# One gelu instruction for two rows' dot products in the expert phase

## The reference, cut to what matters

```
act = gelu(einsum('thkd,td->thk', u[expert], x))      # one dot product per chosen expert
out = einsum('thk,thkd->td', gate * act, v_emb[expert])
```

## Time and profile before

| | |
|---|---|
| median of 3 runs | 3348.26 us (3347.88 to 3351.38) |
| profiled execution | 3351.4 us, of which span 3349.7 us |
| expert phase's first to last row | 745 to 3340 us of the span |
| busy, share of the span | TensorE 82%, VectorE 71%, ScalarE 68%, GpSimd 41% |
| granted TensorE clock, mean | 0.914 |
| gathers (software queue) | 1001 MB, 74.0% of the 16 engines' span |

### The profile page before, as it was taken

The page is one execution under the profiler, slowest core; times in us unless marked ns, Lnnn a source line. Parts: engine busy times, 40 slices in busy tenths (PEclk is TensorE's granted clock), DMA queues, the critical chain, the costliest instruction groups (busy, mean ns, idle before and its releaser), DMA issues.

```text
span 3349.7 us, 47831 instructions
## 1 busy us (share of the span) xinstructions
PE 2730.9 (82%) x16625; PEld 2067.2 (62%) x16625; DVE 2386.9 (71%) x5661; ACT 2272.8 (68%) x4096; POOL 1388.5 (41%) x1158
## 2 busy tenths in 40 slices
PE   8999989889987887787778677776688878878985
PEld 6777667765665664554665454555566658767654
DVE  5554445466788985676776667899988899877556
ACT  3222553236778886786987777767888886887777
POOL 0000100034544553444544443445456654566764
PEclk9999999999999899889789889998899987897997
DMA  3001143149999999999999999999999998999998
GB/s 115 25 33 38 64 139 126 63 164 408 417 418 420 411 415 420 420 414 420 418 407 420 420 415 420 411 418 398 419 365 384 372 359 306 348 400 390 407 399 321
DMA packets 198354, 1099.19 MB, mean 328 GB/s; under 512 B 33767, under 2 KB 49415, under 8 KB 77704
## 3 DMA queue, kind: packets, MB, share of 16 engines
q0 software_dynamic: 152064, 1001.19, 74.0%
q1 hardware_dynamic: 46050, 94.97, 7.9%
HBM read 1173.94 MB, written 11.54 MB: 354 GB/s over the span
## 4 chain that ended last, share of the span: by engine, by line
DMA 24%; DVE 16%; PE 15%; ACT 14%; issue 7%; POOL 2%; DVEq 0%; POOLq 0%; ACTq 0%
DMA early_rows<-in_uv,choice_index 12%; PE expert_acc L3539 7%; DVE scores L3045 5%; DMA rows<-in_uv,expert_sk 3%; ACT early_rows L3231 3%; DMA early_rows<-in_uv,expert_sk 3%; ACT rows L3231 3%; DMA rows<-in_uv,choice_index 2%; DMA rows<-in_uv,scores 2%; DVE early_rows L3045 2%; ACT expert_wt L3225 2%; ACT L3223 2%; DMA early_rows<-in_uv,scores 1%; ACT L1920 1%; ACT expert_wt L3223 1%
## 5 line engine op out<-in xcount | busy, mean ns | idle before, releaser
L3539 PE MATMUL expert_acc<-ident,rows 128*128 128x128 f32 x4072 | 622.1, 305 | 277.7 <-ACT rows L3231 276.2
L3539 PEld LDWEIGHTS expert_acc<-ident,rows 128*128 128x128 f32 x4072 | 524.5, 158 | 471.7 <-ACT rows L3231 421.5
L3539 PE MATMUL expert_acc<-ident,early_rows 128*128 128x128 f32 x4096 | 601.7, 297 | 238.2 <-ACT early_rows L3231 235.8
L3539 PEld LDWEIGHTS expert_acc<-ident,early_rows 128*128 128x128 f32 x4096 | 503.9, 153 | 440.1 <-ACT early_rows L3231 389.4
L3231 ACT ACTIVATE early_rows<-early_rows,expert_wt 128x1024 f32<-128x1024 f32 x512 | 588.6, 1150 | 16.7
L3231 ACT ACTIVATE rows<-rows,expert_wt 128x1024 f32<-128x1024 f32 x510 | 586.2, 1149 | 16.6
L3223 ACT ACTIVATE expert_wt<-expert_dot 128x1 f32<-128x1 f32 x1024 | 202.5, 198 | 484.4 <-DVE expert_dot L3045 479.9
L2029 POOL DMA_INDIRECT rows<-in_uv,choice_index x256 | 317.7, 1241 | 397.1 <-PE expert_acc L3539 353.1
L2029 POOL DMA_INDIRECT early_rows<-in_uv,choice_index x256 | 321.7, 1257 | 338.7 <-PE expert_acc L3539 293.8
L3045 DVE CUSTOM_DVE_ANT_0 rows<-rows,expert_xn 128x1024 f32<-128x1024 f32 x256 | 312.9, 1222 | 149.2 <-DMA rows<-in_uv,choice_index 148.5
L3045 DVE CUSTOM_DVE_ANT_0 early_rows<-early_rows,expert_xn 128x1024 f32<-128x1024 f32 x256 | 312.8, 1222 | 124.1 <-DMA early_rows<-in_uv,choice_index 122.0
(11 more groups left out here) (518 smaller groups left out, 5112.9 us busy)
## 6 DMA issues: line engine op xcount, KB each, us to landing
H<-in_x SPq DMA_DIRECT2D x8, 1024.0 KB, 10.7
expert_w_raw<-in_w_pq SPq DMA_DIRECT2D x16, 512.0 KB, 10.9
stick_w_raw<-in_w_feat SPq DMA_DIRECT2D x8, 512.0 KB, 3.4
tok_w_raw<-in_w_tok SPq DMA_DIRECT2D x8, 512.0 KB, 3.3
out_w_raw<-in_w_out SPq DMA_DIRECT2D x8, 512.0 KB, 3.5
mkv_w_raw<-in_w_mk SPq DMA_DIRECT2D x16, 256.0 KB, 4.0
mkv_w_raw<-in_w_mv SPq DMA_DIRECT2D x16, 256.0 KB, 3.0
pq_w_raw<-in_w_mq SPq DMA_DIRECT2D x8, 512.0 KB, 3.4
```

The source lines that it names most:

```text
L3539: last_mm = nc.tensor.matmul(acc[:, k * P:(k + 1) * P], rows[R % ROWS][:, D + k * P:D + (k + 1) * P], co.ident[:, :], start=b >= dense.FIR ...
```

## The change

For rows below 1020 the gelu is issued at even rows alone, for two neighbouring columns of the dot tile, and it waits until both dot products are there. The Copy with the gate and the scaling of the row stay one for each row. The last four rows are done as before. All else is untouched.

```diff
-                        act.wait_ge(dots, TOPK * g + r + 1)
-                        link(nc.scalar.activation(wt[:, s, 0, r:r + 1], dot[:, s, r:r + 1], ACT.Gelu))
                         R = TOPK * g + r
+                        pairs = R < NB * BLOCK - 4
+                        if not pairs or r % 2 == 0:
+                            n = 2 if pairs else 1
+                            act.wait_ge(dots, R + n)
+                            link(nc.scalar.activation(wt[:, s, 0, r:r + n], dot[:, s, r:r + n], ACT.Gelu))
                         link(nc.scalar.activation(wt[:, s, 1, r:r + 1], wt[:, s, 0, r:r + 1], ACT.Copy,
                                                   scale=row_gate[:, r:r + 1]))
```

## The result

The changed kernel takes 3429.23 us (median of 4 runs, 3426.35 to 3433.81); the kernel before, on the same chip, 3349.77 (3347.88 to 3351.38). The ratio is 1.0241, 95% interval 1.0229 to 1.0253: slower by 79 us, where 8 were forecast.

The account below looks back on a forecast made before the run. DMA bounds 745 to 2460 us and from 2900, ScalarE and VectorE to 2700, VectorE to 2900. Terms 1 + 0 + 0 + 4.4 + 2 + 0.75 = +8.2 on 3348.3 give 3356 us; range 3341 to 3371.

Parts of the forecast that it names:

- the cover: 745 to 1000 us: the DMA covers most of VectorE's added waiting for TensorE's scores; +1 us, ends 0 and +11.
- 1000 to 2460: Stretch with a 14.4 us queue, shortened by 2 us: nothing on the path; 0, from -2 to +4 us.
- 2460 to 2700: Stretch with ScalarE 89% busy: VectorE's wait at L2848 stays as it is; 0, ends -11 and +18 us.
- the turn of the ring: From 2460 us, in the upper bounds only: 1.4 us of lateness for every eight rows, +18 in 2460 to 2700.
- rival C: 2460 to 3100 us: the ring's turn limits wherever the queue is short; +24 us, 3372; chance 0.13.
- 2700 to 3100: Two stretches with longer L2908 waits: +4.4 us up to 2900, then +2 with the DMA hiding the greater part.
- The end: Last rows: row 1020's gelu and the sum's copy come later, nothing parallel; +0.75 us, ends 0 and 1.5.
- The pair's price: ScalarE's gelu of two columns costs 0.20 us, like a single column's; bounds 0.19 and 0.30.
- one pair of table loads fewer: At about 1550 us one pair of ScalarE's table loads falls away, 2.6 us under the DMA; counted as nothing.
- the size of L2908's wait: 2700 to 3100 us: seven L2908 waits each 1.46 us longer, 4.4 us up to 2900 and 5.8 after.
- the sign: Whole kernel: the change makes it slower, by 8.2 us in sum.
- The gain: ScalarE saves 112 us, nearly all beside idle time; at most 11 us could count, in 2460 to 2700.

Follow-up runs that it names:

- ring7: The kernel before with a ring of seven rows instead of eight, single gelus; 3387.14 us, ratio 1.0107.
- pair_relaxed: The changed kernel with four of VectorE's interposed jobs due one or two rows later; 3394.59 us, ratio 1.0138.
- bare: The kernel before and the changed kernel, both without the stick-breaking arithmetic of rows 2 to 200; rows 0 to 192 take 507.3 and 510.9 us.
- relaxed: The kernel before with four of VectorE's interposed jobs due one or two rows later; 3345.99 us, ratio 0.9994.
- odd_pairs: The changed kernel with pairs beginning at odd rows, rows 0 and 15 of each 16 single; 3425.86 us, ratio 1.0234.
- side_first: The changed kernel with ScalarE's interposed work at even rows ahead of the wait for both dot products; 3457.94 us, ratio 1.0319.
- pair_0_448: The changed kernel with pairs in rows 0 to 447 only; 38.4 us late at row 192 and 55.7 at row 448.
- wait_only: The changed kernel with its wait for both dot products but one single-column gelu for each row; 3442.3 us, ratio 1.0269.
- pair_448_736: The changed kernel with pairs in rows 448 to 735 only; +5 us against the kernel before.
- pair_736_1020: The changed kernel with pairs in rows 736 to 1019 only; +20 us against the kernel before.
- bare_single: The kernel before, single gelus, without the stick-breaking arithmetic of rows 2 to 200; rows 0 to 192 take 507.3 us.

## Why the prediction was wrong

**The step that failed** is the cover: "The gathers keep 414 GB/s through those waits today, so the DMA covers most: +1", and for 1000 to 2460 us "a queue of 14.4 us shortened by 2 us stays 12 us long, nearly five rows. Nothing is on the path: 0". By row 96 after is 19.7 us late, by row 640 48.8.

The queue did shorten by 2 us (14.4 to 12.0; in 745 to 1000, where the prediction had no such number, from 11.0 and 10.7 to 9.8 and 9.9), but two things the step held apart work together. The queue's 12 us is a median. And the lateness that shortens it also makes VectorE stand, during which no row is used up and no gather issued. The timeline of after shows two such chains, from row 4 on (start, duration, engine, line; the lines between are left out):

```profile
754.33 1.22 DVE L3045 CUSTOM_DVE_ANT_0 rows<-rows,expert_xn 128x1024 f32<-128x1024 f32 x1 [1.28 <-DMA rows<-in_uv,choice_index]
755.59 0.20 ACT L3227 ACTIVATE expert_wt<-expert_dot 128x2 f32<-128x2 f32 x1 [4.13 <-DVE expert_dot L3045]
759.14 0.49 PE L3437 MATMUL expert_side<-expert_above,ident 128*128 128x128 f32 x2
759.66 0.70 ACT L3147 ACTIVATE expert_w_raw<-expert_side 128x640 f32<-128x640 f32 x1 [2.36 <-PE expert_side L3437]
760.40 0.50 DVE L2935 TENSOR_SCALAR expert_w_raw<-expert_w_raw 128x640 f32<-128x640 f32 x1 [1.29 <-ACT expert_w_raw L3147]
...
764.92 0.09 DVE L3045 DVE_READ_ACCUMULATOR2_ANT expert_dot<- 128x1 f32 x1
773.52 0.69 DVE L2927 TENSOR_TENSOR scores<-expert_acc,rstd 128x512 f32<-128x512 f32 x1 [8.50 <-PE expert_acc L3421]
776.54 0.20 ACT L3227 ACTIVATE expert_wt<-expert_dot 128x2 f32<-128x2 f32 x1 [10.73 <-DVE expert_dot L3045]
781.14 0.99 POOL L2029 DMA_INDIRECT early_rows<-in_uv,choice_index  x1 [8.49 <-PE expert_acc L3542]
```

The pair's gelu waits for row 5's dot product of 754.33. VectorE loses 1.29 us at L2935, with no wait there in the kernel before: it waits for ScalarE's tanh L3147, and that for TensorE's L3437 of 759.14, which before started at 756.99. This lateness comes from row 0. TensorE in after, and then in before:

```profile
747.18 1.97 PE L3542 MATMUL expert_acc<-ident,early_rows 128*128 128x128 f32 x8 [6.68 <-ACT early_rows L3234]
748.94 3.62 PE L3412 MATMUL expert_acc<-z_b,mix_b 128*128 128x512 f32 x4
```

```profile
748.11 2.49 PE L3409 MATMUL expert_acc<-z_b,mix_b 128*128 128x512 f32 x4
```

Row 0 is scaled 3.56 us after its own dot product where before it was 2.02, which is the wait for row 1, 1.54 us. TensorE starts on it after 6.68 us without work (before 5.14), and its granted clock is 0.52 from 747 to 753 (before 0.67 from 746 to 751; 1.00 behind that in both), so the four matmuls behind row 0 take 3.62 us for 2.49. TensorE then works without a gap, and its step for L3147 is late by both, 2.85 us by its distance from row 0's dot product.

The second chain is longer. An even row's dot product is there at 765.00, but its gelu comes at 776.54, since before its partner's turn VectorE stands 8.50 us for TensorE's scores (before, 6.37 us at the same place, with row 8 already on its way). GpSimd waits 8.49 us for that row's slot and issues at 781.14. The kernel before, same row: gelu and gather.

```profile
765.03 0.20 ACT L3223 ACTIVATE expert_wt<-expert_dot 128x1 f32<-128x1 f32 x1 [1.13 <-DVE expert_dot L3045]
...
773.06 0.99 POOL L2029 DMA_INDIRECT early_rows<-in_uv,choice_index  x1 [2.56 <-PE expert_acc L3539]
```

So the lateness of a row is 1.4 to 2 us only where its partner follows at the rows' pace. Where VectorE's own wait lies between the two, the row bears all of it, here 11.5 us, and the queue with it. The forecast took the size of the one for all.

How much that costs in the queue can be counted from the packets, rows 8 to 640 (my count: time with so many gathers issued and not yet landed, and the bytes moved in it; the 25 us of before that are missing lie nearly all at seven):

```
gathers outstanding        0     1     2     3     4     5     6
before  us                 -     -    42   229   425   565   410
        GB/s               -     -   390   405   412   420   420
after   us                 6    42   188   454   596   419    38
        GB/s              27   270   356   406   416   420   419
```

Against 420 GB/s throughout, before loses 20 us in these rows and after 70: the difference of 50 is the 48.8 us by which row 640 is late. So up to there the loss is bytes not moved while three gathers or fewer stood in the queue.

**Which of the two it is.** Shorter queue with the old stalls: +37 (ring7). Longer hand-offs moved out of the way in part: +46 (pair_relaxed). Hand-offs largely absent, queue 2 us shorter but from a deeper level: +3.6 (bare, rows 0 to 192, where the full kernels differ by 30). Fewer stalls with the old queue: nothing (relaxed). Up to row 448 the short queue alone costs 12.6 of the 51 us, and moving the takers gives 22 of them back with pairs and nothing with single gelus (51.0 to 28.9; 0.6): there the one counts through the other, and that is shown. From row 640 on the short queue alone costs 26.8 where pairing costs 28.5, and yet moving the takers leaves 12.0, so the two can't be added up there. How the 79 splits between them is open. Longer hand-offs with a queue held as long as before's were not run.

**A rival that goes along: TensorE's clock.** TensorE stands longer for ScalarE's scalings (561 us over the phase, before 512), and its granted clock falls in the first 192 rows. There it counts. From row 96's dot product to row 192's it takes 255.2 and 254.8 us at a granted clock of 0.88 (after, odd_pairs) but 260.5 to 265.4 at 0.83 to 0.85 (pair_relaxed, side_first, pair_0_448, wait_only), though after and pair_0_448 are the same code up to there. Before takes 244.8 at 0.94. With single gelus, relaxed takes 248.9 at 0.88, so at one clock about 6 of after's 10 us are left in this stretch. In rows 192 to 448 the clock is alike (0.87 and 0.88) and 21 us are lost all the same. So the clock adds to the loss and doesn't make it; no run holds it fixed, and its share of the 30 us of rows 0 to 192 is open.

**The other terms.** 2460 to 2700, forecast 0: rows 640 to 736 lose 9.3 us in the profile and pair_448_736 measures +5, inside the bounds given (up to +18). ring7 loses 9.7 us in these rows without a longer hand-off: the turn of the ring is enough for it, which the prediction had in its bounds and in rival C, but at nothing in its sum. 2700 to 3100, forecast +6.4: rows 736 to 896 lose 18.8, and pair_736_1020 measures +20. There the step named the right wait and its size: L2908 goes from 10.8 to 21.7 us in these 400 us, +10.9, where 4.4 and 5.8 were worked out, and pair_relaxed, in which that wait is 1.5 us, loses 8.4 us in these rows in place of 18.8. What it left out is the ring again: ring7, with no more waiting at L2908 than before (7.9 us), loses 12.8 there. And of the 5.8 the DMA was to hide the greater part, while the gathers of 2900 to 3100 fell from 393 to 349 GB/s. In 1000 to 2115, forecast 0, the seven largest waits for other engines (L2935, L2953, L2959, L2965, L2978, L3001, L3007) grow from 30.8 to 107.0 us together, and none was priced. The end, forecast +0.75: nothing. ScalarE at the end of after, to set beside the earlier trace rows:

```profile
3406.63 0.20 ACT L3227 ACTIVATE expert_wt<-expert_dot 128x2 f32<-128x2 f32 x1 [3.42 <-DVE expert_dot L3045]
...
3409.62 0.19 ACT L3227 ACTIVATE expert_wt<-expert_dot 128x1 f32<-128x1 f32 x1
...
3412.91 1.02 ACT L3238 ACTIVATE expert_hb<-expert_acc 128x1024 f32<-128x1024 f32 x1
```

From the gelu behind row 1019's dot product to row 1020's gelu it is 2.99 us, 0.50 more than in the earlier trace rows, but the sum's copy comes after 6.28, there 6.29: row 1021's gelu had been waiting 0.47 us, and that took it up.

**What held.** The pair's price (0.20 us), one pair of table loads fewer, the size of L2908's wait, and the sign. The gain was small as said: about 13 us of the 127 that ScalarE saved (wait_only against after). Rival C was the nearest. It let the ring's turn count from 2460 to 3100 us, at +24, and in these rows (640 to 896) after loses 28 and ring7 22.5; but 49 of the 77 us were lost ahead of that, by the mechanism that neither it nor the forecast had. Where the range's bounds came from single rows' lateness (+11 for 745 to 1000, +4 for 1000 to 2460), they were too narrow, because they took one lateness of 1.4 us at each wait, and the waits themselves lie inside it.

The Trainium skill, Perfetto Trace Analysis, section Optimizing Scalar/DVE Operations, says that where ScalarE or VectorE isn't saturated but leaves other engines idle, breaking up instructions may let work be done sooner. The runs agree, and narrow it: some 92 us of loss belong to the wait for the second input, which is there with the instructions left single too.

## What to carry to other kernels

Merging two instructions for two items moves the first item's whole tail behind the second's input. Price that against every hand-off between the engines that is issued behind this tail, also in stretches that seem bound by the DMA. Here two stretches at a DMA share of 1.01 lost 13 and 29 GB/s: the share says that the queue is not empty, not that it can lose two more microseconds and bear longer stalls as well. And cut the profile by items, not by times: the fall of TensorE's clock in the first 192 rows, and the place where the short queue alone is enough, show only so. Before counting an edit as covered, count how long the queue already stands at its short end, and what each waiting engine holds back meanwhile.

## What the runs showed of the hardware

The rate of the 1 MB gathers goes with how many are outstanding: 270 GB/s with one (42 us of one trace), 356 to 390 with two, 405 and 406 with three, 412 to 416 with four, 419 to 420 with five or six (the count above). And the bytes did not need TensorE's clock: bare_single moved 418 GB/s in its first 255 us at a granted clock of 0.89 and 420 in the next 290 at 0.70, before 414 at 0.96.
